# Expert gather with the selection matrix as the stationary operand, PE work of an item grouped by array shape, the slot weight moved into the scatter matrix, and five weight tiles of the second item with memory of their own

## What is computed

```python
xt = rms_norm(x, g_ffn).reshape(N, D)                      # 256 x 1024
logits = xt @ w_router + b_router                           # 32 experts
top_v, top_e = lax.top_k(logits, TOP_K)                     # 4 experts a token
wts = jax.nn.softmax(top_v, axis=-1)
...
def expert_block(args):                                     # rows of one expert
    hdn = xblk @ w_mlp1[e] + b_mlp1[e]                      # 1024 -> 2048
    x_glu = jnp.minimum(hdn[:, ::2], SWIGLU_LIMIT)
    x_lin = jnp.clip(hdn[:, 1::2], -SWIGLU_LIMIT, SWIGLU_LIMIT)
    act = x_glu * jax.nn.sigmoid(SWIGLU_ALPHA * x_glu) * (x_lin + 1.0)
    return act @ w_mlp2[e] + b_mlp2[e]                      # 1024 -> 1024
...
y = jnp.zeros((N + 1, D)).at[slot_tok].add(yb * slot_w[:, None])[:N]
return x + y
```

## Time and profile before

| | us |
|---|---|
| median of 3 runs | 1314.65 (1312.81 to 1316.94) |
| the profiled execution, its own time | 1311.81 |
| its span, first to last instruction | 1310.0 |
| PE busy | 1281.5 (98%) |
| DVE, ACT, POOL busy | 395.8, 227.9, 13.6 |
| HBM read | 450.99 MB, 345 GB/s over the span |

### The profile page before, as it was taken

The page is one execution under the profiler, slowest core; times in us unless marked ns, Lnnn a source line. Parts: engine busy times, 40 slices in busy tenths (PEclk is TensorE's granted clock), DMA queues, the critical chain, the costliest instruction groups (busy, mean ns, idle before and its releaser), DMA issues.

```text
span 1310.0 us, 16789 instructions
## 1 busy us (share of the span) xinstructions
PE 1281.5 (98%) x6220; PEld 649.3 (50%) x6220; DVE 395.8 (30%) x652; ACT 227.9 (17%) x369; POOL 13.6 (1%) x19
## 2 busy tenths in 40 slices
PE   6999999998999999999999999999999999999998
PEld 4887787875444444444444444444444444444443
DVE  4664656853221111111211122221111111221222
ACT  3444446430000000100000000100100010000001
POOL 0000000000000000000000000000000000000000
PEclk9999999997899999989999899999999899998999
DMA  8544444594799999999999999999999999999974
GB/s 299 197 170 152 155 165 143 168 361 186 307 397 409 398 417 414 403 399 413 418 417 407 391 419 417 418 406 397 415 417 411 397 406 418 416 406 394 419 312 160
DMA packets 95413, 452.36 MB, mean 345 GB/s; under 512 B 7296, under 2 KB 7328, under 8 KB 62560
## 3 DMA queue, kind: packets, MB, share of 16 engines
q1 hardware_dynamic: 93936, 447.77, 86.0%
q0 software_dynamic: 784, 2.38, 0.6%
q10 hardware_dynamic: 672, 1.92, 0.5%
HBM read 450.99 MB, written 1.05 MB: 345 GB/s over the span
## 4 chain that ended last, share of the span: by engine, by line
PE 93%; DVE 3%; ACT 2%; DMA 1%; issue 1%; DVEq 0%; SPq 0%; ACTq 0%
PE PS L1286 35%; PE PS L1294 20%; PE PS L1271 10%; PE PS L1304 5%; PE PS L1115 5%; PE PS L1116 5%; PE PS L1117 4%; PE PS L1347 1%; PE PS L1132 1%; PE PS L1277 1%; PE PS L1279 1%; PE PS L1111 1%; PE PS L1322 1%; PE PS L1320 1%; ACT mix_hi L532 1%
## 5 line engine op out<-in xcount | busy, mean ns | idle before, releaser
L1286 PE MATMUL PS<-merge_raw,XG 128*64 128x512 f32 x1280 | 292.3, 603 | 0.0
L1294 PE MATMUL PS<-hi_raw,AT 128*64 128x512 f32 x768 | 177.6, 612 | 1.2 <-DMA hi_raw<-in_w_mlp 1.2
L1286 PE MATMUL PS<-raw,XG 128*64 128x512 f32 x768 | 178.4, 600 | 0.0
L1286 PEld LDWEIGHTS PS<-merge_raw,XG 128*64 128x64 f32 x1280 | 86.7, 138 | 161.7 <-issue 161.2
L720 DVE TENSOR_SCALAR SG<-misc,PG 128x128 fp32r<-128x128 f32 x66 | 16.9, 287 | 495.3 <-PE PS L1322 495.1
L969 DVE TENSOR_TENSOR X<-X,PS 128x512 f32<-128x512 f32 x120 | 77.1, 684 | 215.4 <-PE PS L1304 215.4
L1294 PEld LDWEIGHTS PS<-hi_raw,AT 128*64 128x64 f32 x768 | 58.2, 146 | 127.9 <-issue 124.2
L1286 PEld LDWEIGHTS PS<-raw,XG 128*64 128x64 f32 x768 | 49.7, 136 | 121.0 <-issue 121.0
L1271 PE MATMUL PS<-SG,xtl 128*128 128x64 f32 x528 | 107.7, 287 | 0.0
L1271 PE MATMUL PS<-SG,xth 128*128 128x64 f32 x528 | 106.6, 285 | 0.0
L728 DVE TENSOR_TENSOR rest<-raw,mix_hi 128x2048 fp32r<-128x2048 f32 x38 | 86.9, 2291 | 57.8 <-ACT mix_hi L532 57.7
(11 more groups left out here) (247 smaller groups left out, 955.2 us busy)
## 6 DMA issues: line engine op xcount, KB each, us to landing
merge_raw<-in_w_mlp SPq DMA_DIRECT2D x160, 1024.0 KB, 9.5
raw<-in_w_mlp SPq DMA_DIRECT2D x128, 1024.0 KB, 10.0
hi_raw<-in_w_mlp SPq DMA_DIRECT2D x96, 1024.0 KB, 8.3
raw<-in_w_in SPq DMA_DIRECT2D x26, 1024.0 KB, 4.9
raw<-in_w_mem_kv SPq DMA_DIRECT2D x4, 1024.0 KB, 5.0
raw<-in_w_out SPq DMA_DIRECT2D x4, 1024.0 KB, 4.9
raw<-in_w_br_moba SPq DMA_DIRECT2D x2, 1024.0 KB, 5.0
raw<-in_w_br_ret SPq DMA_DIRECT2D x2, 1024.0 KB, 4.9
```

Of the source, the lines that this page charges most:

```text
L1286: mm = pe.matmul(PS[h * SL:(h + 1) * SL, n * 512:(n + 1) * 512], XG[:, u, :], ring[u][:, h * D + n * 512:h * D + (n + 1) * 512], start=Fal ...
L1294: mm = pe.matmul(out[n * SL:(n + 1) * SL, :], AT[:, 2 * v + c, :], ring[W1U + v][:, c * D + n * 512:c * D + (n + 1) * 512], start=(v == 0 ...
```

## The change

**Gather.** The selection `SG` (now fp32, 128 x 64) is the stationary operand and the tokens `hx` themselves move, 512 columns at a time: four products in fp32 (two token tiles, two halves of the width) with a result of 64 rows in each half of bank 3. ACT copies it to `R`; PE transposes `R` with four transposes (`token_transposes`), and DVE copies that into `XG` (`gathered`). The split of the tokens (ACT L630, POOL L493) and their wait are gone.

**Slot weight.** `SS` is now (slot equals position) times the token's weight `gi`, in one DVE instruction; `slotw`, its product L1322, its copy L679 and the wait `slw` are gone.

**Order on PE.** The eight up units, the gather and the down units stand together. After them come scatter transposes of item j-1, token transposes of j+1, activation transposes of j, biases of j+1 and the scatter of j-1, four products to four banks (`scatter_bank`). The scatter thus comes one item late, and the special end with `STL`, `SS2`, `Y2` is gone. DVE adds the four results at the start of its next body.

**Tiles.** Units 0 to 4 of W1 of item 1 get buffers of their own (`early`), in memory that the mixer has left or that held `xth`, `xtl` and others. Units 0 to 4 of W1 of item 2 go to the ring as soon as item 0 has used them. SP's order before its loop is new, and the loop starts at 3.

Cut to its core:

```diff
+        gate_raw = [sb(f"gate_raw{i}", [P, 2048]) for i in range(2)]
+        prob_raw = sb("prob_raw", [P, 2048])
+        low_raw = sb("low_raw", [P, 2048])
+        early = gate_raw + [prob_raw, low_raw, mT[:, :, :].rearrange("p k s -> p (k s)")]
...
+        def weight_tile(j, u):
+            if isinstance(j, int) and j == 1 and u < len(early):
+                return early[u], early_in[u], 16
+            return ring[u], ring_in[u], 16 * (j + 1 if isinstance(j, int) and j < 2 or u >= len(early) else j)
+        def scatter_bank(t, n):
+            return banks[(7, 3, 2, 6)[2 * t + n]]
...
+            def early_left(u):
+                if u <= 1:
+                    sp.wait_ge(y_done, 4)
+                elif u == 2:
+                    sp.wait_ge(b1l, 1)
+                elif u == 3:
+                    sp.wait_ge(unit_used, N_MIX)
+                else:
+                    sp.wait_ge(logits_done, TT)
...
+                    elif isinstance(j, int) and j == 1 and u < len(early):
+                        early_left(u)
+                    elif isinstance(j, int) and j == 2 and u < len(early):
+                        sp.wait_ge(up_used, u + 1)
...
-            load_w1(0, slice(0, 1))
-            load_w2(0, slice(0, 1))
-            load_w1(1, slice(1, 2))
+            load_w1(0, first, range(5))
+            load_w1(1, second, range(3))
+            load_w1(0, first, range(5, W1U))
+            load_w2(0, first)
+            load_w1(1, second, range(3, len(early)))
+            load_w1(2, third, range(len(early)))
+            load_w1(1, second, range(len(early), W1U))
+            load_w1(2, third, range(len(early), W1U))
+            load_w2(1, second)
...
-            with sp.Fori(2, n_items) as j:
+            with sp.Fori(3, n_items) as j:
...
-                pool.tensor_tensor(xtl[:, t, :], hx[:, t, :], xth[:, t, :].bitcast(F32), ALU.subtract).then_inc(xl_done, 1)
-                                act.activation(xth[:, i, :], hx[:, i, :], ACT.Copy).then_inc(xh_done, 1)
...
-            def gathered(i):
+            def gathered_rows(i):
                 act.wait_ge(ga_pe, i + 1)
-                act.activation(XG[:, :, :], banks[6].rearrange("p (k s) -> p k s", s=SL), ACT.Copy).then_inc(xg, 1)
+                act.activation(R[:, :], banks[3], ACT.Copy).then_inc(rows_act, 1)
...
             def body(j):                                    # ACT
-                later = not isinstance(j, int)
-                if later:
-                    output_rows(j - 2)
-                act.wait_ge(st_pe, j + 1)
-                if later:
-                    scatter_matrix(j - 2)
-                if later or j >= 1:
-                    act.wait_ge(swi, 4 * j)
-                act.activation(slotw[:, :], banks[7][:, S:S + 1], ACT.Copy).then_inc(slw, 1)
+                later = not isinstance(j, int) or j >= 1
                 act.wait_ge(swi, 4 * j + 1)
                 act.activation(sig, glu, ACT.Sigmoid, scale=ALPHA).then_inc(sgm, 1)
-                gathered(j + 1)
+                gathered_rows(j + 1)
+                if later:
+                    output_rows(j - 1)
+                    scatter_matrix(j - 1)
                 activations(j)
...
-                    dve.tensor_scalar(SS[:, t, :], slotn, posi[:, t, bass.ds(i, 1)], None, ALU.is_equal).then_inc(ss_mat, 1)
+                    dve.tensor_scalar(SS[:, t, :], slotn, posi[:, t, bass.ds(i, 1)], gi[:, t, bass.ds(i, 1)],
+                                      ALU.is_equal, ALU.mult).then_inc(ss_mat, 1)
+            def gathered(i):
+                dve.wait_ge(xt_pe, i + 1)
+                dve.tensor_copy(XG[:, :, :].rearrange("p (h c) s -> p h c s", h=2),
+                                banks[4].rearrange("p (c h s) -> p h c s", h=2, s=SL)).then_inc(xg, 1)
...
-                dve.scalar_tensor_tensor(act_t, lin, slotw[:, 0:1], sig, ALU.mult, ALU.mult).then_inc(swi, 1)
+                dve.tensor_tensor(act_t, lin, sig, ALU.mult).then_inc(swi, 1)
...
-                for k in range(KC):
-                    for part, xt in enumerate((xth, xtl)):
-                        for t in range(TT):
-                            mm = pe.matmul(banks[6][:, k * SL:(k + 1) * SL], xt[:, t, k * P:(k + 1) * P], SG[:, t, 0:SL],
-                                           start=(part == 0 and t == 0), stop=(part == 1 and t == 1))
+                for t in range(TT):
+                    for n in range(2):
+                        mm = pe.matmul(banks[3][n * SL:(n + 1) * SL, :], SG[:, t, :], hx[:, t, n * 512:(n + 1) * 512],
+                                       start=(t == 0), stop=(t == 1))
                 mm.then_inc(ga_pe, 1)
+            def token_transposes(i):
+                pe.wait_ge(rows_act, i + 1)
+                for c in range(4):
+                    mm = pe.transpose(banks[4][:, c * P:(c + 1) * P], R[:, c * P:(c + 1) * P], ident)
+                mm.then_inc(xt_pe, 1)
...
+                    for v in range(W2U):                    # PE, body(j), after gather(j + 1)
+                        down(j - 1, v)
+                    scatter_transposes(j - 1)
+                token_transposes(j + 1)
                 pe.wait_ge(swi, 4 * (j + 1))
                 for c in range(4):
-                    mm = pe.transpose(banks[3][:, c * P:(c + 1) * P], act_t[:, c * P:(c + 1) * P], ident)
+                    mm = pe.transpose(banks[5][:, c * P:(c + 1) * P], act_t[:, c * P:(c + 1) * P], ident)
                 mm.then_inc(tr_pe, 1)
+                biases(j + 1)
+                if later:
+                    scatter(j - 1)
```

More of the change, by code:

```diff
@@ L1015, in body @@
             def body(j):
-                later = not isinstance(j, int)
-                if later:
-                    dve.wait_ge(st_pe, j)
-                    scatter_matrix(j - 2)
+                looped = not isinstance(j, int)
+                if looped:
+                    for q in range(4):
+                        add(j - 2, q)
                 else:
@@ L1282, in up @@
             def up(j, u):
-                pe.wait_ge(ring_in[u], 16 * (j + 1))
+                tile, landed, count = weight_tile(j, u)
+                pe.wait_ge(landed, count)
                 for n in range(2):
@@ L1306, in body, with scatter @@
+            def scatter(i):
+                pe.wait_ge(yc, i + 1)
+                pe.wait_ge(st_act, i + 1)
+                for t in range(TT):
+                    for n in range(2):
+                        rows = slice(n * SL, (n + 1) * SL)
+                        pe.matmul(scatter_bank(t, n), ST[rows, t * P:(t + 1) * P], Y[rows, :], start=True, stop=True).then_inc(sc_pe, 1)
             def body(j):
-                later = not isinstance(j, int)
+                looped = not isinstance(j, int)
+                later = looped or j >= 1
```

173 lines of the change are left out of this document (62 added, 111 removed).

## The result

The changed kernel takes **1259.67 us** (median of 4 runs, 1257.99 to 1261.28) where the kernel before takes 1315.80 in the same session (4 runs). The ratio is 0.958, 95% interval 0.955 to 0.960: faster, by 4.2%. The forecast was 1260. The profiled execution took 1257.99 us, with a span of 1256.2.

The account below looks back on a forecast made before the run. PE was the bound, with the DMA engines within 2% and due to take over. Start 343.5, 359 tiles 901, latency 2.3 and end 12 gave a span of 1258.8 us; with 1.8 more 1260.6, forecast 1260, range 1250 to 1272.

Parts of the forecast that it names:

- The bound moves to the transfers: Whole kernel: PE and DMA stand within 2% of each other, so a faster PE hands the bound to the DMA engines.
- PE's item, 27.2 us: PE's work per item at full clock: 29.4 - 1.97 - 0.34 - 0.5 + 0.59 = 27.2 us.
- 3.0 us of slack an item: Items from 3 on: PE at 27.2 us has 3.0 us to spare against 30.2 us of transfers.
- The clock: PE in the items: without the old gather, clock 1.00 where it averaged 0.95, which had cost 1.3 us an item.
- The rival in which PE's waits or the block of ten transposes make the clock fall: PE's items: 8 us at half clock gives 1313 us; chance 0.05 still faster (with other waits), 0.04 slower.
- The start: Before the loop: up products of item 0 begin at 306, of item 1 at 331; its sixth unit is done about 343.5 us.
- No gap behind it: Transfers from 343.5 us on: no wait of SP outlasts the backlog, so 359 tiles move in a row, 901 us.
- The end, 12 us: After the last tile's landing: item 30's scatter, DVE's additions and four late down tiles take 12 us (10 to 16).
- The sum: Whole span: 343.5 + 901 + 2.3 + 12 = 1258.8 us, forecast as a time of 1260 us.
- The worth of the early tiles: Before the loop: five tiles loaded early, 2.51 us each, use the DMA engines' idle time from 300 to 315 us.
- they bring nothing: Start of the transfers: SP's new order leaves engines idle as before, 12.6 us more, 1273; chance 0.08, later start included.
- The queue's rate: Transfers in the loop: 417 GB/s taken; a rival had a deeper queue give 424, time 1246, chance 0.12.

## Why the prediction was right, point by point

- **The bound moves to the transfers**: right, shown from both sides (four added products cost next to nothing, two tiles fewer an item gave 88 us).
- **PE's item, 27.2 us**: 26.56. The gather was priced right (1.72). Grouping was under-priced: I took -0.5 us, and the up stretch of 13.88 (14.33 before), down of 6.87 (7.02) and scatter of 1.92 (2.12) come to 0.8 less. Each group of four transposes costs 0.44, not 0.59, for the token transposes that I added and for the activation transposes that were there before. None of it is on the path.
- **3.0 us of slack an item**: 3.0 by the edge found, but by two errors that cancel. I had set a rate of 30.2 against an item of 27.2; the edge is 29.56, since PE's chain has its own start and end, and the item is 26.56.
- **The clock**: full in the loop, as forecast, and the suspicion on the gather holds. The rival in which PE's waits or the block of ten transposes make the clock fall is out: PE waits in every item and the clock is 1.00. The Trainium skill, *TensorE: Matmul & The Clock Gate*, section HAM oscillation, had that rival's rule, but for waits that are longer than the work between them. Here they are 0.54 and 0.56 us beside units of 1.94, so this trace does not test the rule; it shows that waits this short, four or five an item, leave the clock at 1.00.
- **The start**: up of item 0 at 302.55 where I had 306. Half of that is an earlier first gather, 297.66 for 301.67, 4.0 us where I had 2.2: beside `oh`, `nv` took 0.15 us and not 1.37. The other half is that this gather ran at full clock, 1.89 us for 6.67. The chance of the trace is in it, too: in the eight with a late start, up of item 0 begins at 303.8 to 306.1, near where I had it. From there to up of item 1 it took 21.4 us where I had 25. DVE's `oh` took 0.49 us for 2.64. So the sixth unit of item 1 was done at 336.6 and not at 343.5: 6.9 us early.
- **No gap behind it**: not quite. The stream fell to 307 GB/s between 345 and 348 us and to 369 between 357 and 360. At 343.70 SP issued the first W2 tile of item 1, which waits for the down products of item 0, with only three tiles issued since 336.6, and at 354.96 the first W1 tile of item 3, which waits for the first up unit of item 2. The first wait I had not seen, the second I had put at 362. The last landing came at about 1242 us, 2.1 later than 336.6 + 2.3 + 901 = 1239.9. The 417 GB/s were right.
- **The end, 12 us**: 14.2. PE waited for the additions, which I had in the sum, then did four units that start only at 1242.0, and the last additions and the output's DMA came behind a scatter that had to wait 0.7 us for `Y`.
- **The sum**: -6.9 + 2.1 + 2.2 = -2.6, which is 1258.8 against a span of 1256.2. The errors are as large as the early tiles' worth, and their sum is small partly by luck.
- **The worth of the early tiles**: wrong by a factor of three or more where I named it. My own way of counting would have given it: 364 tiles from item 1's first unit, 10.8 us earlier, in place of 359 from its sixth, some 2 us more. The rival "they bring nothing" was priced at 5 x 2.51 = 12.6 us; taking them out costs 2.5 to 3.7. A tile that is moved ahead of one gap is only worth its time if it doesn't open the next. The forecast did not hang on it, since it counted from the last gap on.
- **The queue's rate**: the deeper queue (19 to 25 us to a landing, for 9.9) did not run faster than 417 to 418 GB/s: that rival is out. The Trainium skill, *DMA: Bandwidth & Descriptors*, section Bandwidth, has HBM transfers bound at about 358 GB/s; one core here read at 417 for 880 us, so the measurement decides. The section gives 358 as a core's share when both cores of a domain stream, and its 425 for a core alone; the 417 are within 2% of that, and I should have read the 358 with its condition.

## What to carry to other kernels

When two resources stand within a few per cent, price the change by the other one's remaining work: find the last moment at which it idles, count what is left, add the tail. A slack per item is not the difference of two rates but of two whole chains, each with its own start and end. And tiles moved ahead of a gap are worth what has been moved in all when the gapless stretch begins; fill one gap and read where the next one opens.

## What the runs showed of the hardware that I had not expected

- 32 short fp32r products (128 x 128 stationary, 64 moving columns) an item made PE's clock fall behind them in 13 of 30 items, 1.6 and 3.3 us in the two shown; as many records of short fp32 products (with other operands), of the same length in all, in none.
- A DMA issue on SP took longer in a full queue: with about ten tiles under way (24.8 us to a landing, 2.5 to a tile) single issues of W2 tiles took 4.1 to 4.4 us, and 0.38 where SP had waited for PE just before. It cost nothing here, but SP's waits for PE look shorter by it (84.2 us in all on the W1 tiles of the changed kernel, 433.1 before).
- DVE's two `oh` instructions (`tensor_tensor`, 128 x 128) took 2.64 us beside GpSimd's subtractions and 0.49 without them. They took 2.64 again in the run with the new gather alone, which keeps the subtractions. I had only inferred that from two other instructions of the same shape.
- Two runs of 4 KB in place of one of 8 KB to a partition cost 1% of the rate when the stream is mixed.
